# Rows of the modulation matrix summed earlier on VectorE, and ScalarE's exponential and sigmoid table moved behind group four

## The reference

```python
cond = jax.nn.silu(c)
mod = cond @ w_ada[l] + b_ada[l]
sh1, sc1, gt1, sh2, sc2, gt2 = [m[:, None, :] for m in jnp.split(mod, N_MOD, axis=-1)]
h = rms_norm(x, g_pre_mix[l]) * (1.0 + sc1) + sh1
zin = h @ w_in[l]
cv_val, cv_gate, q, f, i, og = jnp.split(zin, splits, axis=-1)
out_a = conformer_conv(cv_val, cv_gate, ...)   # u = val * sigmoid(gate), conv of 31 taps, ...
out_b = hgrn2(q, f, i, og, lb_all[l], hgrn_norm_g[l])
mix = jnp.concatenate([out_a, out_b], axis=-1) @ w_out[l]
x = x + gt1 * rms_norm(mix, g_post_mix[l])
```

## Time and profile before

| | before |
|---|---|
| median of 3 runs | 1190.41 us (1188.95 to 1190.81) |
| profiled execution, its own time | 1186.35 us |
| its span, first to last instruction | 1184.6 us |
| TensorE busy | 1141.7 us, 96% of the span |
| VectorE busy | 740.9 us, 63% |
| GpSimd busy | 661.9 us, 56% |
| ScalarE busy | 306.1 us, 26% |
| share of TensorE in the chain that ended last | 92% |
| mean granted TensorE clock | 0.996 |

### The profile page before, as it was taken

How to read it: one execution, slowest core, us unless ns; L and a number is a source line. 1 busy time by engine, 2 the same in 40 slices (tenths; PEclk the granted TensorE clock), 3 DMA queues, 4 the chain that set the end, 5 groups by cost and what they waited for, 6 DMA issues and landing times.

```text
span 1184.6 us, 13775 instructions
## 1 busy us (share of the span) xinstructions
PE 1141.7 (96%) x5528; PEld 953.0 (80%) x5528; DVE 740.9 (63%) x893; ACT 306.1 (26%) x460; POOL 661.9 (56%) x388
## 2 busy tenths in 40 slices
PE   2799999999999999999999999999999999999996
PEld 2678888888887888878888888888888888888885
DVE  5776979979988655658744444444444444444447
ACT  5455254272341624341110101010101010101014
POOL 4045434342333460315486868686877777777755
PEclk9999999999999999999999999999999999999999
DMA  9545323232310153202112020202020203020216
GB/s 331 170 130 155 102 77 91 89 89 77 102 36 26 47 206 114 89 25 66 36 36 71 30 77 22 85 20 88 18 89 18 89 19 89 19 89 18 89 40 262
DMA packets 94097, 98.52 MB, mean 83 GB/s; under 512 B 2925, under 2 KB 80978, under 8 KB 94034
## 3 DMA queue, kind: packets, MB, share of 16 engines
q1 hardware_dynamic: 92576, 93.33, 25.0%
q10 hardware_dynamic: 1458, 4.31, 0.9%
HBM read 89.25 MB, written 8.39 MB: 82 GB/s over the span
## 4 chain that ended last, share of the span: by engine, by line
PE 92%; DVE 3%; ACT 1%; SPq 1%; DMA 1%; issue 1%; ACTq 0%; DVEq 0%
PE pair L1716 31%; PE pair L1637 27%; PE pair L1529 24%; PE pair L1565 4%; PE pair L1694 1%; PE pair L1492 1%; DVE acc L959 1%; DMA x<-in_x 1%; SPq L404 1%; PE pair L1579 1%; PE pair L1560 1%; PE pair L1453 1%; PE pair L1441 1%; PE pair L1581 1%; PE pair L1574 1%
## 5 line engine op out<-in xcount | busy, mean ns | idle before, releaser
L1081 DVE SCALAR_TENSOR_TENSOR pair<-u,conv_w_col,pair 128x512 f32<-128x512 f32 x240 | 162.5, 750 | 1.2
L1393 DVE TENSOR_TENSOR yt<-yt,pair 128x1024 f32<-128x1024 f32 x80 | 97.6, 1220 | 95.2 <-PE pair L1637 95.1
L604 POOL TENSOR_TENSOR w_lo<-raw,w_hi 128x1024 fp32r<-128x1024 f32 x66 | 146.6, 2222 | 5.3
L602 POOL CAST w_hi<-raw 128x1024 fp32r<-128x1024 f32 x66 | 68.6, 1040 | 121.2 <-PE pair L1637 52.5
L525 POOL TENSOR_TENSOR w_lo<-raw,w_hi 128x1024 fp32r<-128x1024 f32 x21 | 52.4, 2499 | 104.6 <-ACT w_hi L689 104.6
L1637 PE MATMUL pair<-w_hi,u_hi 128*128 128x512 f32 x352 | 108.6, 390 | 0.3 <-DVE yt L1391 0.3
L1637 PE MATMUL pair<-w_lo,u_hi 128*128 128x512 f32 x352 | 108.4, 389 | 0.0
L1637 PE MATMUL pair<-w_hi,u_lo 128*128 128x512 f32 x352 | 108.4, 389 | 0.0
L604 POOL TENSOR_TENSOR w_lo<-sraw,w_hi 128x1024 fp32r<-128x1024 f32 x38 | 104.3, 2744 | 3.0
L602 POOL CAST w_hi<-sraw 128x1024 fp32r<-128x1024 f32 x38 | 39.5, 1039 | 117.7 <-PE pair L1637 116.0
L536 POOL TENSOR_TENSOR acc<-acc,ada 128x1024 f32<-128x1024 f32 x28 | 67.4, 2406 | 52.4 <-ACT ada L733 51.1
(11 more groups left out here) (259 smaller groups left out, 2583.5 us busy)
## 6 DMA issues: line engine op xcount, KB each, us to landing
ada<-in_w_ada SPq DMA_DIRECT2D x48, 512.0 KB, 3.9
raw<-in_w_ffn_in SPq DMA_DIRECT2D x44, 512.0 KB, 3.9
raw<-in_w_in SPq DMA_DIRECT2D x24, 512.0 KB, 3.9
raw<-in_w_ffn_out SPq DMA_DIRECT2D x22, 512.0 KB, 3.4
x<-in_x SPq DMA_DIRECT2D x8, 512.0 KB, 8.4
raw<-in_w_out SPq DMA_DIRECT2D x8, 512.0 KB, 3.4
x<-in_x SPq DMA_DIRECT2D x4, 1024.0 KB, 8.1
out<-x ACTq DMA_DIRECT2D x8, 512.0 KB, 2.6
```

The lines of the kernel that those rows point to most:

```text
L602: me.done(pool.tensor_copy(w_hi[:, g % WS, cols], src[:, cols]))
L604: pool.tensor_tensor(w_lo[:, g % WS, cols], src[:, cols], w_hi[:, g % WS, cols], ALU.subtract).then_inc(w_split, 1)
L1081: i_ = dve.scalar_tensor_tensor(out=dst, in0=src, scalar=w, in1=dst, op0=ALU.mult, op1=ALU.add)
L1393: dve.tensor_tensor(yt[:, i, :], yt[:, i, :], pair[2 + n % 2][:, :], ALU.add).then_inc(y_added, 1)
```

## The change

On VectorE rows of blocks two and three are summed earlier than before, against the low halves. The instructions are the same; only the order of the calls of `sum_rows`, `low_half` and `scale_shift` changes. On ScalarE the exponential for the lower bounds, with its wait, moves from behind group 15 to behind group 3 (the fourth group), and a load of the sigmoid's table is written behind it.

```diff
             for g in range(16):
                 full_and_high(g)
-
-
-            act.wait_ge(vec_ready, 2)
-            act.activation(lb_tmp[:, 1, :], lb_tmp[:, 0, :], ACT.Exp).then_inc(cond_ready, 1)
+                if g == 3:
+                    act.wait_ge(vec_ready, 2)
+                    act.activation(lb_tmp[:, 1, :], lb_tmp[:, 0, :], ACT.Exp).then_inc(cond_ready, 1)
+                    act.preload_act_table_set("sigmoid_and_others")
+
             act.wait_ge(vec_ready, 3)
...
             scale_shift(3)
-            sum_rows(2, range(2, 4))
+            sum_rows(2, range(2, 6))
             low_half(4)
-            sum_rows(2, range(4, 6))
+            sum_rows(2, range(6, KT))
             low_half(5)
-            sum_rows(2, range(6, KT))
+            sum_rows(3, range(2))
             low_half(6)
             scale_shift(4)
+            sum_rows(3, range(2, 4))
             low_half(7)
-            sum_rows(3, range(3))
             scale_shift(5)
+            sum_rows(3, range(4, 6))
             low_half(8)
-            sum_rows(3, range(3, 6))
+            sum_rows(3, range(6, KT))
             low_half(9)
-            sum_rows(3, range(6, KT))
             low_half(10)
```

## The result

Six runs of the changed kernel took 1180.73 to 1182.6 us, median 1181.01; six of the kernel before, 1185.93 to 1190.81, median 1188.83. The ratio is 0.9939, 95% interval 0.9928 to 0.9951: **7.3 us faster, between 5.8 and 8.6** (the two medians lie 7.8 us apart; the us given for a ratio are its share of the median of before). Forecast were 4.5 us and 1185.9 us, with a range whose lower end was 1183.8. The two profiled executions differ by 5.1 us (1186.35 and 1181.24, spans 1184.6 and 1179.5). So there are two things to explain: 5.1 instead of 4.5 between the profiles, and another 2 us between the medians.

A forecast was written before the change was run, and what follows sets the result against it. TensorE, busy 96% of the span, was taken to bound the kernel, so only its waits could be won: 1.93 (block two) + 1.27 (block three) + 1.30 (sigmoid) = 4.50 us, 1190.41 to 1185.9 us, range 1183.8 to 1188.7.

The forecast's parts named there:

- The three stalls: TensorE's waits for block two, block three and the sigmoid before the first projection: 1.93, 1.27 and 1.30 us saved.
- The idle times left: TensorE's remaining idle: 0.4 us before block two's sum, 0.4 before block three's, 0.6 before the first projection.
- the 0.64 us wait of scale 5: VectorE in block three: scale 5 waits for tile 5's block sum with rows 4 and 5 queued behind, 0.7 us forecast.
- the two table loads in ScalarE's idle time: ScalarE before group 4: exponential and both loads, 2.8 us, fit into 8.27 us of idling and cost nothing.
- the lower bounds in time: VectorE behind low half 15: four small instructions, 0.8 us, done 0.5 us ahead of the sigmoid's start.
- The new wait of 0.2 us for group 8's low half: TensorE in block three: group 8's products wait some 0.2 us for VectorE's low half, a stall not there before.
- The sum's last step: The 4.50 us saving, a difference of waits, is carried over from the profile to the median: 1190.41 - 4.50 = 1185.9 us.
- half-speed stretch: Rival: a half-speed stretch of TensorE falls on 8 products, costing 1.6 us; saving 2.9, 1187.5 us; chance 0.10.
- more than forecast: Rival: the whole sigmoid and block three stalls go, no new group 8 wait; saving 5.7, 1184.7 us; chance 0.05.
- given back: Rival: the earlier start is lost in the later projections to VectorE's taps or a transfer; saving 0 to 2; chance 0.06.
- The range: Whole kernel's median forecast between 1183.8 us (1184.7 - 0.9) and 1188.7 us (1187.5 + 1.2).
- The table: ScalarE before the first projection: sigmoid starts 1.30 us earlier without its load; the Trainium skill's figure would give 2.66 us.

The follow-up runs named there:

- before_full: Kernel before plus unused 128x512 products in TensorE's four waits (6, 9, 7 for blocks one to three, 7 before the first projection): 1185.76 us, ratio 0.9979.
- after_fill: Changed kernel plus six unused 128x512 products on TensorE in the wait for block one: 1181.59 us, ratio 0.9939 to the kernel before.
- turn_first: Changed kernel with TensorE's turns of group 4 ahead of group 3's products, sums of blocks two and three asked later, VectorE's rows fitted: 1180.52 us, ratio 0.9930.
- before_fill: Kernel before plus six unused 128x512 products on TensorE in the wait for block one: 1188.54 us, ratio 0.9997; profiled execution 1192.43 us.
- before_again: Kernel before, unchanged, profiled a second time: 1186.95 us, span 1185.2 us.
- b3_only: Kernel before with only block three's rows summed earlier on VectorE: 1185.50 us, one execution.
- v_only: Kernel before with VectorE's new order of rows alone, exponential and sigmoid's table left behind group 15: 1183.91 us, ratio 0.9959.
- s_only: Kernel before with ScalarE's part alone, exponential and sigmoid's table load behind group 3, VectorE's order as before: 1185.88 us, ratio 0.9971.
- b2_only: Kernel before with only block two's rows summed earlier on VectorE: 1183.96 us, one execution.
- before: Kernel before, unchanged; its first profiled execution took 1186.35 us, span 1184.6 us.
- s_full: Kernel before with ScalarE's part alone plus 6, 9 and 7 unused products in TensorE's waits for blocks one, two and three: 1185.30 us, ratio 0.9973.

## Why the prediction was wrong

- **The three stalls: right.** 1.93, 1.27 and 1.30 us were forecast, and the runs show 1.92, 1.26 and 1.30 against the execution of before that was free of half-speed stretches up to there. The idle times left, the 0.64 us wait of scale 5, the two table loads in ScalarE's idle time and the lower bounds in time are all as laid out. The new wait of 0.2 us for group 8's low half shows only in the starts: its first product stands 0.58 us behind the start of the turns ahead of it (50.00 to 50.58), where it was 0.36 (52.49 to 52.85).
- **The sum's last step: wrong.** It said that the saving is a difference of waits and is carried over to the median. The profiled execution of before lay 4.06 us under the median of its three runs and 2.5 us under the median of six; that difference was set aside as if both kernels had it. The changed kernel does not: its profiled execution lies 0.2 us above its median. It was the missing term: in the kernel before, TensorE's waits bring half-speed stretches in many executions, worth 2.5 us of the median (`before_full`, 1.4 to 3.6). The changed kernel has shorter waits and little of it: its profile, `after_fill` and `turn_first` have no stretch there, six fillers changed nothing (ratio 0.9939 with and without), and its six runs lie within 1.9 us. 4.5 + 2.5 = 7.0 us, of 7.3 measured; with these intervals the close agreement is partly luck.
- **Rival "half-speed stretch": the right mechanism with the wrong sign.** Its price, 1.6 us, was right: the 16.40 against 14.80 us above. (It was read from a place where the clock column says 1.00; that the products there ran at half speed is borne out by their 0.43 us, the same as at a clock of 0.50 in `before_fill`.) But it was held against the changed kernel, because the kernel before showed a clock of 1.00 behind its 2.33 us wait. It did so in the one execution that was profiled; five other profiles with such waits (`before_again`, `before_fill`, `b3_only`, `v_only`, `s_only`) show the fall at one wait or another, and one (`b2_only`) shows none.
- **Rivals "more than forecast" and "given back": not it.** The stalls gave 4.5 us and not 5.7, and all of it arrived at the end (1113.4 us behind the first projection in both).
- **The range: too narrow below** for the same reason. Its low end was built from stalls alone.
- **The table: the trace's price held.** With its own part alone, the first projection's wait fell by 1.28 us (1.89 to 0.61). The Trainium skill's 1380 ns of drain beside the load ("ScalarE: Activation LUTs", What ACT_TABLE_LOAD costs), 2.66 us a switch with it, does not show: in the kernel before the sigmoid starts 1.30 us after its load does.

Not settled: what decides, in a given execution, which wait is followed by a half-speed stretch. `before` and `before_again` have the same waits and different places. Nor is it settled how the 2.5 us divide among the four waits, and what makes the five longer executions of `before_full`.

## What to carry to other kernels

Where the median of the runs lies well above the profiled execution, the profile is of a lucky one: look at the clock and the spread of the runs before a saving is carried over, and profile the kernel twice. A wait of TensorE can cost more on average than its length; here three of about 2 us and one of 1.6 us carried 2.5 us on top. To measure that share by itself, fill the waits with products that nobody reads.

## What the runs showed of the hardware

- The granted clock fell to 0.50 (1.2 GHz) at or behind waits of TensorE of 1.1 to 2.3 us, in some executions and not in others, with work on TensorE on both sides: behind 1.11 us in `s_full`, 1.56 in `before`, 1.89 in `before_again` and `v_only`, 2.33 in `b3_only`. Waits of 1.16 and 1.38 us in the profile of the changed kernel were not followed by one. 128x512 products then stand 0.43 instead of 0.23 us apart (48.65 to 49.08 in `before_fill`).
- Such a stretch lasted 3.3 to 3.5 us in these profiles and cost 1.2 to 1.6 us where it fell on products, 0.5 where it fell on the turns of `before`.
- Once, in `before_fill`, it stayed there from 46 to 52.6 us and cost 3.1 us; TensorE was busy all that time.
- Executions also differ by how late the groups start: block one's sum stood at 35.86 us in `before_full` and at 37.10 in `s_full`, whose VectorE order up to there is the same, and at 36.40 and 36.00 in the two profiles of the kernel before.
- A sum over partitions with one column costs TensorE some 0.25 us; the trace has two records for each. Eight sums (16 records) took 1.95 us, four 1.05.
